# Two attentions of an encoder trunk: stacked value columns, denominators behind the second tile, 192 keys and three logit slots

## The reference

```
logits = q k^T / 8 + bias[rel_bucket(k - q)]      # keys: own chunk and the one before
p = softmax(concat(logits, sink))[..., :-1]
out = p v                                          # then a projection
```

## Time and profile before

| | |
|---|---|
| median of the runs | 2831.47 us |
| profiled execution | 2833.7 us |
| its span, first to last instruction | 2831.7 us |
| mean granted TensorE clock | 0.970 |
| first attention | about 488 to 887 us |
| second attention | about 1830 to 2049 us, fills from 1946 |

### The profile page before, as it was taken

How to read it: one execution, slowest core, us unless ns; L and a number is a source line. 1 busy time by engine, 2 the same in 40 slices (tenths; PEclk the granted TensorE clock), 3 DMA queues, 4 the chain that set the end, 5 groups by cost and what they waited for, 6 DMA issues and landing times. The chain is left out here.

```text
span 2831.7 us, 36530 instructions
## 1 busy us (share of the span) xinstructions
PE 2648.8 (94%) x12584; PEld 2156.8 (76%) x12584; DVE 1506.9 (53%) x2879; ACT 1005.4 (36%) x1819; POOL 751.1 (27%) x369
## 2 busy tenths in 40 slices
PE   6899997998998999999999998867989999999998
PEld 5689776776766778888888877656777888888886
DVE  4599999665665653344333453155555334433345
ACT  5443523555553432211222143265643221122212
POOL 2112786333232122222222212311122222222220
PEclk9999988999999999999999999899999999999999
DMA  4461624432435421111111134633442111111113
GB/s 132 70 107 44 159 89 169 122 102 75 144 114 211 150 83 60 45 52 38 58 44 52 45 119 123 153 111 99 123 167 90 53 48 49 45 51 44 52 37 119
DMA packets 260043, 258.17 MB, mean 91 GB/s; under 512 B 11906, under 2 KB 219810, under 8 KB 257620
## 3 DMA queue, kind: packets, MB, share of 16 engines
q1 hardware_dynamic: 250436, 239.22, 29.1%
q10 hardware_dynamic: 9216, 16.78, 2.0%
q0 software_dynamic: 272, 0.62, 0.1%
HBM read 181.60 MB, written 74.97 MB: 91 GB/s over the span
## 5 line engine op out<-in xcount | busy, mean ns | idle before, releaser
L405 PE MATMUL ps<-xn_T,w_split 128*128 128x512 f32 x4608 | 1066.1, 393 | 18.4 <-DVE xn_T L1506 14.2
L405 PEld LDWEIGHTS ps<-xn_T,w_split 128*128 128x128 f32 x4608 | 872.7, 190 | 206.3 <-DVE xn_T L1506 16.7
L362 POOL TENSOR_TENSOR w_split<-w_raw,w_split 128x1024 fp32r<-128x1024 f32 x192 | 464.4, 2429 | 1517.6 <-ACT w_split L355 1517.3
L405 PE MATMUL ps<-w_split,hidden 128*128 128x512 f32 x3648 | 835.0, 390 | 7.2 <-POOL w_split L362 6.2
L405 PEld LDWEIGHTS ps<-w_split,hidden 128*128 128x128 f32 x3648 | 685.8, 188 | 151.4 <-issue 6.6
L1784 DVE TENSOR_TENSOR acc<-acc,ps 128x512 f32<-128x512 f32 x504 | 344.5, 687 | 333.6 <-PE ps L405 333.5
L355 ACT ACTIVATE w_split<-w_raw 128x1024 fp32r<-128x1024 f32 x192 | 197.7, 1050 | 600.8 <-PE ps L405 591.7
L1794 DVE TENSOR_TENSOR sq_h<-relu_h 128x512 f32<-128x512 f32 x128 | 88.6, 692 | 509.9 <-ACT relu_h L1332 509.9
L1332 ACT ACTIVATE relu_h<-ps 128x512 f32<-128x512 f32 x128 | 76.7, 599 | 454.6 <-PE ps L405 451.8
L1731 DVE TENSOR_TENSOR probs_T<-ps,probs_T 128x512 fp32r<-128x512 f32 x204 | 140.5, 690 | 155.3 <-ACT probs_T L1289 154.8
L405 PE MATMUL ps<-probs_T,v_split 128*64 128x512 f32 x612 | 192.0, 423 | 22.2 <-DVE probs_T L1731 21.7
(11 more groups left out here) (164 smaller groups left out, 2126.1 us busy)
## 6 DMA issues: line engine op xcount, KB each, us to landing
w_raw<-in_w SPq DMA_DIRECT2D x128, 512.0 KB, 3.9
q_scratch<-q_split SPq DMA_DIRECT2D x128, 128.0 KB, 2.4
q_tile<-q_scratch ACTq DMA_DIRECT2D x64, 256.0 KB, 2.6
cat_scratch<-attn_out_split SPq DMA_DIRECT2D x128, 128.0 KB, 2.4
w_raw<-in_w_in SPq DMA_DIRECT2D x30, 512.0 KB, 4.4
unit_tile<-cat_scratch SPq DMA_DIRECT2D x48, 256.0 KB, 3.5
h_scratch<-acc SPq DMA_DIRECT2D x24, 512.0 KB, 4.6
h_in<-h_scratch SPq DMA_DIRECT2D x24, 512.0 KB, 5.8
```

Source lines behind the costliest of these rows:

```text
L362: nc.gpsimd.tensor_tensor(whl[:, n0 % 4, 1, :], wraw[:, n0 % 4, :], whl[:, n0 % 4, 0, :].bitcast(F32), ALU.subtract).then_inc(w_lo, 1)
L405: return nc.tensor.matmul(out_ap, stat, mov, start=start, stop=stop)
```

## The change

- **Both attentions.** The value tile is stored as [128 keys, 128 columns], 64 high columns and 64 low ones side by side. One matmul gives high x p in partitions 0 to 63 of bank 6 and low x p in 64 to 127. A tile takes two matmuls (p high, p low) with 128 stationary columns in place of three with 64 (low x low is now included). Denominators are spread over 128 partitions, and DVE multiplies twice, once for each half of the bank. The sum of the halves is made with the split: the high part is a copy of the first half, and the low part takes two POOL steps, (first half - high) + second half.
- **First attention.** The denominators move behind the second key tile's transposes (the first one's for b = 0) and take their turn between logits 1 and 2. ACT's high copy of the result moves behind the first `probs_T` copy of the next block. POOL adds mask to bias three blocks ahead. DVE inverts the sums before the first subtraction.
- **Second attention.** It gets functions of its own. Keys are 192 (the tile's own 128 and the odd chunk before it). Logits take turns in three banks, 0 to 2; denominators have bank 3. Three logits of the next block are issued ahead. The odd chunk has 64 rows: its high part goes to partitions 0 to 63 and its low part to 64 to 127, with the values of the chunk held twice (`vodd`), and one matmul does both. ACT makes its four exps in a row and then the denominators' copy. All three steps of the split of the result are POOL's.
- **SP** handles fills before the spill of the same block.

```
-    v2b = at("v_split1", [P, 2, 2, NB, HD], F32R, XT0 + 56 * K)
+    v2b = at("v_split1", [P, 2, NB, 2, HD], F32R, XT0 + 56 * K)
+    vodd = at("v_odd_chunk", [P, 2, NB, 2, HD], F32R, XT0 + 33 * K)
...
+    def l_logits(b, j):        # first attention
+        return 5 * b - 1 + j + (j >= 2)
...
+    # PE, first attention
+            vv = v2[:, kt, :, :].rearrange("p l d -> p (l d)")
+            mm(ps[:, 6, :], vv, pT[:, q % 4, 0, :], st == 0, False)
+            mm(ps[:, 6, :], vv, pT[:, q % 4, 1, :], False, st == keys[b] - 1).then_inc(pv_done, 1)
...
                     last.then_inc(c_full, 1)
+                    if st == 0 and todo:
+                        logits(i, b + 1, todo.pop(0))
+                    if st == min(1, keys[b] - 1):
+                        denominators(i, b, last_step)
+                    if st and todo:
+                        logits(i, b + 1, todo.pop(0))
                     if st:
                         values(i, b, st - 1)
...
+    # DVE, end of a block, first attention
+                dve.wait_ge(ol_ok, CREDIT + b - 1 + 8 * i)
+                nc.vector.tensor_tensor(osb[:, s, :], ps[0:HD, 6, :], rec[0:HD, s, :], ALU.mult).then_inc(o_high, 1)
+                nc.vector.tensor_tensor(olo[:, s, :], ps[HD:P, 6, :], rec[HD:P, s, :], ALU.mult).then_inc(o_ok, 1)
...
+    def pe_attn1(pe):           # second attention
+        for g in range(HG * NB):
+            for _ in range(LEAD1 if todo else 0):
+                logits(g + 1, todo.pop(0))
+            for k in fills:
+                fill(pe, fu1, T_O1, k, 0, 2)
+            pe.wait_ge(e1_ok, 4 * g + 4)
+            q = T_BASE1[g]
+            if b:
+                transposes(g, slice(0, CHUNK), q)
+                q += 1
+            transposes(g, slice(CHUNK, CHUNK + P), q)
+            denominators(g)
+            for j in todo:
+                logits(g + 1, j)
+            if g:
+                pe.wait_ge(o1_ok, g)
+            if b:
+                pe.wait_ge(t1_free, q)
+                mm(o, value_pair(vodd[:, kv], b - 1), pS1[:, s, :], True, False)
+            for k in fills:
+                fill(pe, fu1, T_O1, k, 2, 4)
+            pe.wait_ge(t1_free, q + 1)
+            mm(o, value_pair(v2b[:, kv], b), pL1[:, s, 0, :], b == 0, False)
+            mm(o, value_pair(v2b[:, kv], b), pL1[:, s, 1, :], False, True).then_inc(o1_full, 1)
...
+    # DVE, one block of the second attention
+            for _ in range(LEAD1 if todo else 0):
+                logits(g + 1, todo.pop(0))
+            dve.wait_ge(e1_ok, 4 * g + 4)
+            nc.vector.reciprocal(rinv[:, s, :], rsum[:, s, :]).then_inc(r1_ok, 1)
+            if g % NB:
+                probs_low(pS1[HD:P, s, :], ps[0:HD, 4 + q % 2, :], pS1[0:HD, s, :], q)
+            for j in todo:
+                logits(g + 1, j)
+            probs_low(pL1[:, s, 1, :], ps[:, 4 + q % 2, :], pL1[:, s, 0, :], q)
+            for k in FILL[1][divmod(g, NB)]:
+                take_fill(k)
+            dve.wait_ge(o1_full, g + 1)
+            dve.wait_ge(d1_free, g + 1)
+            if g >= 2:
+                dve.wait_ge(s1_ok, g - 1)
+            # two multiplies: olo1 from ps[HD:P], osb1 from ps[0:HD]
...
+    # ACT, one block: copies of one or two tiles, then
+                for j in range(4):
+                    exps(g + 1, j)
+            act.wait_ge(d1_full, g + 1)
+            nc.scalar.activation(rec1[:, s, :], ps[:, 3, :], ACT.Copy).then_inc(d1_free, 1)
...
+    def pool_attn1(pool):       # one block
+            pool.wait_ge(o1_ok, g + 1)
+            pool.wait_ge(o_sp[s], 16 + 512 + 32 * (g // 2))
+            nc.gpsimd.tensor_copy(ohl1[:, s, 0, :], osb1[:, s, :]).then_inc(s1_hi, 1)
+            nc.gpsimd.tensor_tensor(osb1[:, s, :], osb1[:, s, :], ohl1[:, s, 0, :].bitcast(F32), ALU.subtract).then_inc(s1_rest, 1)
+            nc.gpsimd.tensor_tensor(ohl1[:, s, 1, :], osb1[:, s, :], olo1[:, s, :], ALU.add).then_inc(s1_ok, 1)
```

More of the change, by code:

```diff
@@ L912, in pool_program, with pool_attn0 @@
         pool_ffn(pool, LAYERS[1])
[L914 to L926, removed]
+    def pool_attn0(pool):
+        pool.wait_ge(at_ld0, 16)
+        pool.wait_ge(ao_sp, 16 * GROUPS)
+        pool.wait_ge(mask_ok, 2)
         def mask_bias(i, b):
@@ L1237, in act_program @@
             act.wait_ge(a_full, f + 1)
-            for kv in range(2):
-                last = nc.scalar.activation(v2b[:, kv, 0, 4 * k:4 * k + 4, :],
-                                            ps[:, f % 4, :].rearrange("p (b e d) -> p b e d", b=4, e=2)[:, :, kv, :], ACT.Copy)
+            tiles = ps[:, f % 4, :].rearrange("p (b e d) -> p e b d", b=4, e=2)
+            nc.scalar.activation(v2b[:, :, 4 * k:4 * k + 4, 0, :], tiles, ACT.Copy)
+            for half in range(2):
+                last = nc.scalar.activation(vodd[half * HD:(half + 1) * HD, :, 4 * k:4 * k + 4, 0, :], tiles[HD:P], ACT.Copy)
             last.then_inc(a_hi, 1)
         split_hi(act, T_O1 + 3)
-        act_attn(act, 1, C_TOT0)
+        act_attn1(act)
         act_out(act, LAYERS[1])
@@ L1637, in dve_program @@
             dve.wait_ge(a_hi, hi_count["sm1"] + k + 1)
-            for kv in range(2):
-                last = lo(v2b[:, kv, 1, 4 * k:4 * k + 4, :], ps[:, f % 4, :].rearrange("p (b e d) -> p b e d", b=4, e=2)[:, :, kv, :],
-                          v2b[:, kv, 0, 4 * k:4 * k + 4, :])
+            cols = slice(4 * k, 4 * k + 4)
+            tiles = ps[:, f % 4, :].rearrange("p (b e d) -> p e b d", b=4, e=2)
+            lo(v2b[:, :, cols, 1, :], tiles, v2b[:, :, cols, 0, :])
+            for half in range(2):
+                last = lo(vodd[half * HD:(half + 1) * HD, :, cols, 1, :], tiles[HD:P], vodd[HD:P, :, cols, 0, :])
             last.then_inc(a_free, 1)
-        dve_attn(dve, 1, C_TOT0)
+        dve_attn1(dve)
         dve_out(dve, LAYERS[1])
@@ L2043, in body @@
                 if "end" in fills:
-                    fill(*fills["end"])
-                denominators(i, b, last_step)
+                    fill0(*fills["end"])
                 values(i, b, keys[b] - 1)
-        for j in range(4):
-            logits(0, 0, j)
-        pe.wait_ge(l_full, base_l + l_logits(0, 3) + 1)
+        logits(0, 0, 0)
+        logits(0, 0, 1)
+        pe.wait_ge(l_full, L_BASE + l_logits(0, 1) + 1)
         pe.sem_inc(l_full, 1)
+        logits(0, 0, 2)
+        logits(0, 0, 3)
```

462 lines of the change are left out of this document (267 added, 195 removed).

## The result

The changed kernel took 2813.85 us (median of 4 runs, 2809.75 to 2815.9) where the kernel before took 2832.12 on the same chip (4 runs, 2831.44 to 2833.86): ratio 0.993, 95% interval 0.9915 to 0.9946. It is faster by 18 us. The prediction said 43 and a range of 2764 to 2812; the time lies just outside it. The profiled execution of the kernel after took 2815.9 us around a span of 2814.1.

The account below looks back on a forecast made before the run. PE was taken to bound the first attention and the part with fills, a chain of waits the part without. Terms -26 + 1.3 + 0.7 - 1 - 14 + 0.7 - 5.5 + 1.0 = -42.8 gave 2789 us; range 2764 to 2812.

Parts of the forecast that it names:

- Denominators move from the block's end to behind its second tile: First attention: ACT's copy releases the next block's exps earlier, 3 us gained in all; bounds 1 lost to 6 gained.
- The mask sum ... and the reordered SP work have slack: First attention: POOL, busy 126 of 399 us, takes the earlier mask sum and a second result step without cost.
- The rest of the first attention: First attention: fewer value matmuls on PE gain 5.8 us per head group, 23 in all, built up by block length.
- The wider value loads: Value matmuls: loading 128 columns instead of 64 costs nothing; starts 0.23 us apart, or 0.28 if the load shows.
- Rival A: First attention: DVE becomes the bound and the gain is only 10 us, 2805 in all; chance 0.10.
- rival C: Bank 6: PE's next values wait for both multiplies, so the kernel gets slower, +16 us, 2848; chance 0.08.
- 5.14: Second attention, blocks 1 to 15 without fills: us from multiply to multiply through DVE, against 6.43, gaining 19 us before clock loss.
- the best of all bounds: Whole kernel: first attention -39, no clock drops and no new wait would give 2757 us.
- rival B: Second attention without fills: clock stays at 1.2 GHz through most of it, gaining 3 instead of 14, 2800; chance 0.10.
- Hand-over: Second attention, blocks 16 and 17: the first fill's unit loads wait for later spills, +0.7 us.
- forecast 6.3: Second attention, 14 blocks with fills: 6.3 us each instead of 6.7, with 0.7 idle before the odd value matmul; -5.5.
- The tail's +1.0: After the last block: POOL's weight splits start 2.5 us later, 1.5 of it slack, so 1.0 us lost.

Follow-up runs that it names:

- experiment 1: Kernel after with the first attention's denominators back at the block's end: 2797.27 us, ratio 0.9873.
- experiment 2: Kernel before with only the first attention's denominators moved behind the second key tile and sums inverted before the first subtraction: 2855.65 us, ratio 1.0076.
- experiment 9: Experiment 1 plus GpSimd's weight splits ahead of its result steps at the end of the second head group only: 2790.31 us, ratio 0.9852.
- experiments 3 and 5: 3: kernel after without the first attention's second multiply, 2814.49 us; 5: the same left out of experiment 1, 2797.93 us.
- experiments 4 and 10: 4: kernel after plus three unused matmuls per block without fills, 2812.68 us; 10: that, experiment 6, experiment 9 and fills from block 18 in one kernel, 2773.95 us.
- experiment 6: Kernel after with the odd chunk's value matmul behind the second half of the fill in the second attention: 2804.24 us, ratio 0.9895.

## Why the prediction was wrong, step by step

**The step that failed: "Denominators move from the block's end to behind its second tile ... 3 us in all (bounds: 1 us lost ... to 6 gained)".** The move costs 18.2 us (experiment 1, taken back) to 23.4 us (experiment 2, made alone). I had the mechanism half in hand: the lower bound names DVE's third logits waiting for the copy. I priced one engine's late release and not the turn. The denominators use a slot in a ring of two, so for one step the ring has one slot, and PE and DVE, which otherwise work on different heads, alternate. Against experiment 1 that is 1.0 to 1.8 us in each of the blocks b=2 to b=4 and 0.1 to 0.9 in those with b=5 and 6. At the block's end the same four transposes cost less: DVE has read all four heads by then, and the next logits find a free slot. The trace of before could have shown it: in its block 20 one logits slot takes 1.27 us of DVE and 0.7 to 0.8 of PE, and with one slot they add.

**"The mask sum ... and the reordered SP work have slack: POOL is busy 126 of 399 us".** True on average, wrong in block 17. GpSimd's steps for the result stood ahead of two weight splits that a fill waits for. One more step, and ACT's later copy in front of it, made block 17 4.8 us longer than before while block 16 got 2.6 shorter. Blocks 16 and 17 together took 16.5 us before, 18.7 after and in experiment 1, and 13.3 in experiment 9, with the splits first. An average of a third says nothing of the one block in 32 where a queue is full.

**The rest of the first attention: the sum came out, its parts did not.** With the denominators and the splits put where they cost nothing (experiment 9), blocks 0 to 31 took 357.0 us, 26.8 less than before, and some 4 of that may be the odd block 23 of before. My sum without the denominators' 3 was -23. But it was built up by block length, and there the multiplies say something else. Gains in us, four head groups together:

```
                                   b=0   b=1   b=2   b=3   b=4   b=5   b=6   b=7    sum
forecast                             0   0.4   1.2   2.0   4.0   5.2   6.0   4.4   23.2
experiment 9 against before        3.3   1.6   0.7   2.1   1.1   2.7   1.2  14.1   26.8
```

Blocks b=4 to b=6 brought 5.0 us where I had 15.2, and b=7 with b=0 brought 17.4 where I had 4.4. That these two misses cancel is luck. For b=4 the timeline of block 20 in the kernel before has the reason: DVE's heads already stood 1.89 us apart there, as in experiment 1, so matmuls saved on PE do not shorten that part of the block.

```profile
729.58 0.68 DVE L1687 CUSTOM_DVE_ANT_0 logits<-ps,masks 128x512 f32<-128x512 f32 x1
...
731.47 0.68 DVE L1687 CUSTOM_DVE_ANT_0 logits<-ps,masks 128x512 f32<-128x512 f32 x1
```

The gain at b=7 is mostly not PE's. Block 31 went from 16.3 to 11.8 us in the kernel after, and block 15 from 16.2 to 12.5. Before, ACT's high copy and two weight splits stood between the multiply of block 30 and the first `probs_T` copy of block 31:

```profile
870.45 0.68 DVE L1745 TENSOR_TENSOR attn_out<-ps,rec_den 64x512 f32<-64x512 f32 x1 [1.01 <-PE ps L405]
...
871.70 1.99 ACT L355 ACTIVATE w_split<-w_raw 128x1024 fp32r<-128x1024 f32 x2
...
873.59 1.06 ACT L1289 ACTIVATE probs_T<-ps 128x512 fp32r<-128x512 f32 x2
...
874.95 0.96 PE L405 MATMUL ps<-probs_T,v_split 128*64 128x512 f32 x3 [3.66 <-DVE probs_T L1731]
```

After:

```profile
870.41 0.68 DVE L1776 TENSOR_TENSOR attn_out<-ps,rec_den 64x512 f32<-64x512 f32 x1 [0.83 <-PE ps L414]
...
870.84 0.60 ACT L1297 ACTIVATE probs_T<-ps 128x512 fp32r<-128x512 f32 x1
...
872.80 0.73 PE L414 MATMUL ps<-probs_T,v_split 128*128 128x512 f32 x2
```

The copy starts 0.43 us behind the multiply instead of 3.14, and the first value matmul 2.4 us behind it instead of 4.5. The move of ACT's high copy is a part of the change to which my sum gave no term. The rest of the block fell from 11.8 to 9.4 us; before, it ran partly at 1.2 GHz. The whole of block 31, before and after (the clock is the third number from the end):

```profile
870.45:886.76 16.31, 12.17 (x60) 7.87 (x58) 6.18 (x10) 7.66 (x12) 5.96 (x3) 0.90 0.52 178
```

```profile
870.41:882.22 11.81, 9.14 (x52) 6.28 (x50) 6.99 (x12) 6.10 (x11) 7.26 (x4) 1.00 0.64 222
```

No experiment takes ACT's move back alone, so what it is worth by itself stays open. The turn of two tiles did fall as forecast, from 2.77 us to some 2.6 (875.38 to 877.97 in block 31 of the kernel after).

**The wider value loads: not quite nothing.** The stated test was 288 value matmuls 0.23 us apart, and 0.28 if the load shows. Where PE has not waited it holds: in experiment 1 two of them start 0.47 us ahead of what follows (723.91 to 724.38). Behind a wait the load shows. Three value matmuls before, from block 30, and two after, from block 31:

```profile
863.44 0.91 PE L405 MATMUL ps<-probs_T,v_split 128*64 128x512 f32 x3 [0.44 <-DVE probs_T L1731]
864.19 0.60 PE L2035 MATMUL ps<-ident,logits 128*128 128x128 f32 x4
```

```profile
875.38 0.73 PE L414 MATMUL ps<-probs_T,v_split 128*128 128x512 f32 x2 [0.51 <-DVE probs_T L1764]
875.95 0.60 PE L2106 MATMUL ps<-ident,logits 128*128 128x128 f32 x4
```

With 0.23 for each but the first, the first took 0.28 to 0.29 before and takes 0.34 after. It is so in all the groups behind a wait at 2.4 GHz: 0.28 or 0.29 in the 27 of before, 0.33 or 0.34 in the 36 of after. That is 0.06 x 36 = 2 us of PE time, by estimate. The Trainium skill, "TensorE: Matmul & The Clock Gate", section "LDWEIGHTS (loading the stationary operand)", makes a load's time P/1.2 ns for P columns: an estimated 0.05 us for 64 more, and some 20 us if every load showed. The trace agrees with the 0.05 behind a wait and not elsewhere, where the load of 128 columns lies under the matmul before it.

**Rival A, "DVE becomes the bound", and rival C, bank 6.** Both put the loss on the second multiply, and taking it away changed nothing (experiments 3 and 5). DVE's added work is not what made the short blocks longer: DVE waits for logits there. A's time (2805) was nearer than mine, for a reason that is not its own.

**Second attention without fills, "5.14".** The block took 5.50. Read off one block of the kernel after in my own terms, the excess is in four hand-overs: the multiplies until the first logits 1.32 instead of 1.21, reciprocal to denominators 0.31 instead of 0.21, logits pair until DVE starts 0.63 instead of 0.45, and 0.05 behind the subtract; the logits were 0.07 cheaper:

```profile
1886.71 0.69 DVE L1842 TENSOR_TENSOR attn_out_low<-ps,rec_den 64x512 f32<-64x512 f32 x1 [0.83 <-PE ps L414]
...
1888.03 0.40 DVE L1803 CUSTOM_DVE_ANT_0 logits<-ps,bias,neg_sinks 128x192 f32<-128x192 f32 x1
...
1889.04 0.17 DVE L1829 RECIPROCAL prob_inv<-prob_sums 128x4 f32<-128x4 f32 x1
...
1889.35 0.62 PE L2163 MATMUL ps<-ident,prob_inv 128*128 128x128 f32 x4 [1.15 <-DVE prob_inv L1829]
...
1889.73 0.45 PE L414 MATMUL ps<-k_split,q_tile 128*128 128x192 f32 x2
...
1890.36 0.42 DVE L1803 CUSTOM_DVE_ANT_0 logits<-ps,bias,neg_sinks 128x192 f32<-128x192 f32 x1 [0.44 <-PE ps L414]
...
1891.45 0.74 PE L414 MATMUL ps<-probs_T_tile,v_split 128*128 128x512 f32 x2 [0.91 <-DVE probs_T_tile L1811]
...
1892.23 0.69 DVE L1842 TENSOR_TENSOR attn_out_low<-ps,rec_den 64x512 f32<-64x512 f32 x1 [0.84 <-PE ps L414]
```

The chain's path was the one I had written down. (Its terms add to 5.12, not 5.14; and the best of all bounds, as they stand in the prediction, gives 2762, not 2757.) It brought 15 x 0.36 = 5 us less than priced; the clock cost 3 instead of 5. Net -11.1 for -14.

**The clock, rival B.** It fell now and then, not for good: 0.88 over the stretch. The fall goes back to PE's missing work: with three matmuls more a block it stays at 2.4 GHz (experiments 4 and 10). The Trainium skill, "TensorE: Matmul & The Clock Gate", section "A second HAM failure mode: psum-queue depth-cycling", has short idle times between groups of matmuls make the clock go to and fro; the trace agrees in kind, and the rows give the size here: 3.1 us in 85.3.

**Hand-over, fills, ends.** PE idled 5.94 us before its first fill where I had said 7, and the hand-over took 2.0 more where I had said 0.7; the kernel after and its siblings took 19.6 to 21.4 for it, the kernel before and experiment 2 19.4 and 18.0, so the difference is hardly more than scatter. The multiply-to-multiply of 6.38 with fills met the forecast 6.3, with the wait before the odd value matmul where I had put it. The tail's +1.0 can't be held to be more than chance: seven of the kernels with the same tail took 780.7 to 782.9 us for it.

## What to carry to other kernels

Before an instruction is moved into a ring of two slots, count how many slots are left to the producer and the consumer while it is there: with one, they alternate, and a step costs the sum of both. Before a queue is given one more step because it is mostly idle, look for the one place where something late waits behind it, and for the one where something waits for that very step; here the same reordering gained 6 us at one end of a head group and lost 6 at the other. When a change carries several moves, the cheapest one on paper deserves its own bound from the timeline: here it took back 18 of the 19 us that the rest of the change had earned in the first attention. And a sum that comes out is checked part by part before it is called right: here blocks of one length gained a third of their forecast and blocks of another three times theirs.

## What the runs showed of the hardware that was not expected

A GpSimd copy of 64x512 values took 0.60 us, where the subtraction of the same shape took 1.26: from the GpSimd queue of the kernel after, one block of the second attention.

```profile
1921.64 0.60 POOL L970 CAST attn_out_split<-attn_out 64x512 fp32r<-64x512 f32 x1 [2.07 <-DVE attn_out L1843]
1922.32 1.26 POOL L972 TENSOR_TENSOR attn_out<-attn_out,attn_out_split 64x512 f32<-64x512 f32 x1
```

The idle time in front of a matmul understates what its wait costs, since the matmuls before it are recorded 0.17 us longer than the distance at which the next could start (0.45 against 0.28, experiment 6). And unused PE work can be worth adding: three matmuls of 512 columns per block, 0.7 us of PE time each block, made the blocks shorter by keeping the clock up.
